# Ten of 32 adaLN blocks moved from the conv-FFN stages into five gaps between stages

## The reference

```python
c_act = jax.nn.silu(c)
for l in range(DEPTH):
    mod = c_act @ ada_w[l] + ada_b[l]                 # 1024 x 6144 for each of 2 layers
    sh1, sc1, gt1, sh2, sc2, gt2 = [m[:, None, :] for m in jnp.split(mod, 6, axis=-1)]
    h = rms_norm(x, norm1_g[l]) * (1.0 + sc1) + sh1
    ...
```

## Time and profile before

| | us |
|---|---|
| median of 3 runs | 2023.67 (2022.28 to 2025.08) |
| profiled execution, its own time | 2017.43 |
| its span | 2015.7 |
| PE busy | 1856.9 (92%) |
| DVE busy | 1292.1 (64%) |
| ACT busy | 1025.2 (51%) |
| granted clock of PE, mean | 0.957 |
| one pair in the conv-FFN loops, from one adaLN block to the next (856.70 to 874.65 on PE) | 17.95 |
| products in a row, start to start (874.10, 874.22, 874.33, 874.44 on PE) | 0.113 |
| unit 0 of the LRU ends (ACT's first read of it starts at 605.95) | about 605.7 |

### The profile page before, as it was taken

The page is one execution under the profiler, slowest core; times in us unless marked ns, Lnnn a source line. Parts: engine busy times, 40 slices in busy tenths (PEclk is TensorE's granted clock), DMA queues, the critical chain, the costliest instruction groups (busy, mean ns, idle before and its releaser), DMA issues.

```text
span 2015.7 us, 40167 instructions
## 1 busy us (share of the span) xinstructions
PE 1856.9 (92%) x16293; PEld 1749.0 (87%) x16293; DVE 1292.1 (64%) x1985; ACT 1025.2 (51%) x1550; POOL 29.5 (1%) x48
## 2 busy tenths in 40 slices
PE   6999889999979579999979999889998999988998
PEld 5987879999969569999969899879997999987998
DVE  5845667777757467777765866655555766765554
ACT  5634455555556645555545465434443655444443
POOL 0000000000000000000000000000000000100000
PEclk9996899999989789999989999989999999998999
DMA  7540337777744227777623341225553433043553
GB/s 278 187 146 1 126 110 278 259 268 272 262 160 149 84 103 262 270 270 263 248 105 107 128 163 44 90 99 188 189 194 118 147 137 136 3 147 126 189 189 124
DMA packets 43886, 333.52 MB, mean 165 GB/s; under 512 B 4864, under 2 KB 4992, under 8 KB 5632
## 3 DMA queue, kind: packets, MB, share of 16 engines
q1 hardware_dynamic: 38592, 277.89, 38.3%
q0 software_dynamic: 4608, 50.33, 6.7%
q10 hardware_dynamic: 576, 3.71, 0.5%
HBM read 330.86 MB, written 1.05 MB: 165 GB/s over the span
## 4 chain that ended last, share of the span: by engine, by line
PE 85%; DVE 8%; ACT 4%; issue 2%; DMA 1%; DVEq 0%; ACTq 0%
PE unit L492 15%; PE unit L494 15%; PE unit L493 15%; PE acc L492 8%; PE acc L494 8%; PE acc L493 8%; PE misc L388 2%; PE misc L1328 2%; ACT w_hi L469 1%; PE acc L1420 1%; DVE w_lo L476 1%; DMA par<-par_in 1%; PE misc L1434 1%; DVE tmp L1618 1%; DVE tmp L1654 1%
## 5 line engine op out<-in xcount | busy, mean ns | idle before, releaser
L476 DVE TENSOR_TENSOR w_lo<-raw,w_hi 128x1024 fp32r<-128x1024 f32 x526 | 640.1, 1224 | 473.1 <-ACT w_hi L469 463.2
L469 ACT ACTIVATE w_hi<-raw 128x1024 fp32r<-128x1024 f32 x526 | 555.4, 1062 | 654.0 <-PE unit L494 385.0
L492 PE MATMUL unit<-h_hi,w_hi 128*128 128x256 f32 x2656 | 754.3, 284 | 50.1 <-DVE h_lo L403 32.9
L493 PE MATMUL unit<-h_lo,w_hi 128*128 128x256 f32 x2656 | 746.7, 281 | 0.0
L494 PE MATMUL unit<-h_hi,w_lo 128*128 128x256 f32 x2656 | 746.2, 281 | 0.0
L492 PEld LDWEIGHTS unit<-h_hi,w_hi 128*128 128x128 f32 x2656 | 509.8, 192 | 60.6 <-issue 42.2
L493 PEld LDWEIGHTS unit<-h_lo,w_hi 128*128 128x128 f32 x2656 | 510.7, 192 | 0.2
L494 PEld LDWEIGHTS unit<-h_hi,w_lo 128*128 128x128 f32 x2656 | 510.2, 192 | 0.0
L492 PE MATMUL acc<-mv_hi,w_hi 128*128 128x256 f32 x1360 | 384.7, 283 | 36.1 <-DVE mv_lo L548 36.1
L493 PE MATMUL acc<-mv_lo,w_hi 128*128 128x256 f32 x1360 | 380.2, 280 | 0.0
L494 PE MATMUL acc<-mv_hi,w_lo 128*128 128x256 f32 x1360 | 379.9, 279 | 0.0
(11 more groups left out here) (368 smaller groups left out, 1735.1 us busy)
## 6 DMA issues: line engine op xcount, KB each, us to landing
raw<-w_in SPq DMA_DIRECT2D x263, 1024.0 KB, 4.8
ada_ring<-ada_in POOLq DMA_DIRECT2D x32, 1536.0 KB, 8.5
keep<-gates_in ACTq DMA_DIRECT2D x1, 1280.0 KB, 5.4
par<-par_in ACTq DMA_DIRECT2D x1, 1261.0 KB, 14.6
x<-x_in SPq DMA_DIRECT2D x1, 1024.0 KB, 5.7
out<-x SPq DMA_DIRECT2D x4, 256.0 KB, 2.1
con<-con_in ACTq DMA_DIRECT2D x1, 950.0 KB, 4.7
con<-con_in ACTq DMA_DIRECT2D x1, 130.0 KB, 5.9
```

The lines of the kernel that those rows point to most:

```text
L469: act(half(w_hi, c, k), raw[c % RAW][:, CW // 2 * k:CW // 2 * (k + 1)], ACT.Copy).then_inc(S("high_parts"), 1)
L476: tt(half(w_lo, c, k), raw[c % RAW][:, CW // 2 * k:CW // 2 * (k + 1)], half(w_hi, c, k).bitcast(f32), ALU.subtract).then_inc(S("chunk_spli ...
L492: mm(out, w, m, start=first, stop=False)
L493: mm(out, w, ml, start=False, stop=False)
```

## The change

- Blocks 0 and 1 stand before `ffn0`, 16 and 17 before the LRU, 20 and 21 before `ffn1`, 30 and 31 before `in2_0`: on PE the first of each right behind the `pe_norm` of the result, in `misc[1]` (`pe_gap`), the second behind the `pe_norm` of the next stage's input, in the first bank of `acc` (`pe_gap_end`); on DVE both right behind the last `h_lo` (`dve_gap`).
- Blocks 18 and 19 stand in the LRU, on PE between its last input chunk and the first down chunk, in `misc[0]` and a bank `unit`; on DVE behind the last split of `lru_out`. There `dve_mod(0)` stands too, which was behind `dve_pre` of `ffn1`.
- `ffn0` keeps blocks 2 to 15 (one in each pair of the loop). `ffn1` keeps 22, before the first down chunk, and 23 to 29, one in a loop turn, in its first pair; the second pair has none.
- POOL's loop over loads is written out, with a table of slots (`SLOT`).

```diff
 pe_ffn:
             pe_unit(pe, c0 + 1, n0 + 1)
-            if l == 0:
-                pe.wait_ge(S("c_act"), 1)
-            pe_ada(pe, l, 0)
             for j in range(2):
                 pe_unit(pe, c0 + 2 + j, n0 + 2 + j)
-            pe_ada(pe, l, 1)
+            pe.wait_ge(S("ada_turned"), GAP[f"ffn{l}"] + 2)
+            if l == 1:
+                pe_ada(pe, 22, misc[0])
             pe_down(pe, c0 + 4, b0, True, False)
             with pe.Fori(0, 7) as i:
                 for k in range(2):
                     for j in range(2):
                         pe_unit(pe, c0 + 5 + 3 * k + j, n0 + 4 + 2 * k + j, i, 6, 4)
-                    pe_ada(pe, l, 2 + k, i)
+                    if l == 0:
+                        pe_ada(pe, 2 + k, misc[k], i)
+                    elif k == 0:
+                        pe_ada(pe, 23, misc[1], i, 1)
                     pe_down(pe, c0 + 7 + 3 * k, b0 + 1 + k, False, False, i, 6, 2)
...
 dve_ffn:
+            dve_gap(dve, f"ffn{l}")
             dve.wait_ge(S("unit_free"), U0[f"ffn{l}"] + 2)
...
                 product(2 * p + 1, i)
-                dve_ada(dve, l, p, i)
+                if l == 0 and p >= 2:
+                    dve_ada(dve, p, misc[p % 2], i)
+                elif l == 1 and p == 1:
+                    dve_ada(dve, 22, misc[0])
+                elif l == 1 and p == 2:
+                    dve_ada(dve, 23, misc[1], i, 1)
...
 pe_lru:
             pe_mod(pe, 0)
+            pe_ada(pe, 18, misc[0])
+            pe.wait_ge(S("unit_free"), n0 + 11)
+            pe_ada(pe, 19, unit[n0 % 2])
             pe_out(pe, "lru_out")
...
 dve_lru:
+            dve_gap(dve, "lru")
             dve.wait_ge(S("lam_log"), 1)
...
             dve_out(dve, "lru_out", lru_pair, recur)
+            dve_mod(dve, link, 0)
+            dve_ada(dve, 18, misc[0])
+            dve_ada(dve, 19, unit[n0 % 2])
             done_after(dve, END["lru_out"] - 1)
...
+        GAP = {"ffn0": 0, "lru": 16, "ffn1": 20, "in2": 30}
+        def pe_gap(pe, first, second):
+            n = GAP[second]
+            pe_norm(pe, first)
+            if n == 0:
+                pe.wait_ge(S("c_act"), 1)
+            if n == 20:
+                pe.wait_ge(S("mod_done"), 1)
+            pe_ada(pe, n, misc[1])
+        def pe_gap_end(pe, second):
+            pe_ada(pe, GAP[second] + 1, accb[0])
+        def dve_gap(dve, second):
+            n = GAP[second]
+            dve_ada(dve, n, misc[1])
+            dve_ada(dve, n + 1, accb[0])
...
 tensor program:
-            pe_norm(pe, "mix_post0")
+            pe_gap(pe, "mix_post0", "ffn0")
             pe_norm(pe, "ffn_pre0")
+            pe_gap_end(pe, "ffn0")
             pe_ffn(pe, 0)
```

More of the change, by code:

```diff
@@ L348, in one @@
             return con[0:rows, CON[name]:CON[name] + 1]
+        accb = [acc[:, 512 * b:512 * (b + 1)] for b in range(4)]
         ident, ones = cn("ident"), cn("ones")
@@ L1148, in pe_lru @@
             pe.wait_ge(S("gates_loaded"), 16)
+            pe.wait_ge(S("ada_turned"), 18)
             for k in range(5):
@@ L1307, in ada_load @@
             pool.dma_start(ada_slot[s], src).then_inc(S(f"ada_loaded{s}"), 16)
+        SLOT = [n % 2 for n in range(22)] + [0] + [1] * 7 + [0, 1]
+        TURN = [SLOT[:n].count(SLOT[n]) + 1 for n in range(2 * ADA_N)]
         def pool_ada(pool):
-            for s in range(2):
-                ada_load(pool, s, s)
-            with pool.Fori(0, ADA_N - 1) as i:
-                for s in range(2):
-                    pool.wait_ge(S("ada_rows"), i * 2 + (s + 1))
-                    ada_load(pool, s, i * 2 + (2 + s))
@@ L1319, in pe_ada @@
-        def pe_ada(pe, l, p, i=None):
-            n = ADA_N * l + p
-            pe.wait_ge(S(f"ada_loaded{n % 2}"), at(i, 16, 16 * (n // 2 + 1)))
-            if i is not None or n >= 2:
-                pe.wait_ge(S("ada_turned"), at(i, 2, n - 1))
+            for n in range(2 * ADA_N):
+                s = SLOT[n]
+                if TURN[n] > 1:
+                    before = max(m for m in range(n) if SLOT[m] == s)
+                    pool.wait_ge(S("ada_rows"), before + 1)
+                ada_load(pool, s, n)
@@ L1326, in pe_ada @@
+        def pe_ada(pe, n, bank, i=None, per=2):
+            s = SLOT[n]
+            pe.wait_ge(S(f"ada_loaded{s}"), at(i, 16, 16 * TURN[n]))
+            if i is not None:
+                pe.wait_ge(S("ada_turned"), at(i, per, n - per + 1))
             for k in range(8):
                 g = 32 * (k % 4)
-                ins = mm(misc[n % 2][g:g + 32, 0:ADA_W], cact[:, k:k + 1].to_broadcast([P, 32]),
-                         ada_slot[n % 2][:, k, :], start=(k < 4), stop=(k >= 4))
+                ins = mm(bank[g:g + 32, 0:ADA_W], cact[:, k:k + 1].to_broadcast([P, 32]),
+                         ada_slot[s][:, k, :], start=(k < 4), stop=(k >= 4))
@@ L1330, in pe_ada, with dve_ada @@
             ins.then_inc(S("ada_rows"), 1)
-        def dve_ada(dve, l, p, i=None):
-            n, w = ADA_N * l + p, ADA_W // 32
-            dve.wait_ge(S("ada_rows"), at(i, 2, n + 1))
+        def dve_ada(dve, n, bank, i=None, per=2):
+            w = ADA_W // 32
+            dve.wait_ge(S("ada_rows"), at(i, per, n + 1))
             if i is not None or n >= 1:
-                dve.wait_ge(S("ada_cols"), at(i, 2, n))
-            nc.vector.transpose(ada_turned[:, :], misc[n % 2][:, 0:ADA_W]).then_inc(S("ada_turned"), 1)
-            dve.wait_ge(S("ada_turned"), at(i, 2, n + 1))
-            dst = ada_cols[:, w * n:w * (n + 1)] if i is None else ada_cols[:, bass.ds(i * (2 * w) + w * n, w)]
+                dve.wait_ge(S("ada_cols"), at(i, per, n))
+            nc.vector.transpose(ada_turned[:, :], bank[:, 0:ADA_W]).then_inc(S("ada_turned"), 1)
+            dve.wait_ge(S("ada_turned"), at(i, per, n + 1))
+            dst = ada_cols[:, w * n:w * (n + 1)] if i is None else ada_cols[:, bass.ds(i * (per * w) + w * n, w)]
@@ L1389, in build @@
         oacc = acc8[:, 4:8, :]
-        accb = [acc[:, 512 * b:512 * (b + 1)] for b in range(4)]
         KB = [unit[0][:, :], unit[1][:, :], misc[0][:, :], misc[1][:, :]]
@@ L1424, in pe_b2_in @@
             pe_norm(pe, f"pre1_{l}")
+            if l == 0:
+                pe_gap_end(pe, "in2")
             c0, n0 = CH0[f"in2_{l}"], U0[f"in2_{l}"]
             pe_unit(pe, c0, n0, h_count=4 * HU[f"pre1_{l}"])
+            pe.wait_ge(S("ada_turned"), 32)
             pe.wait_ge(S("mod_done"), l + 1)
@@ L1571, in dve_b2_in @@
             dve_modulated(dve, link, f"pre1_{l}", l, 0)
+            if l == 0:
+                dve_gap(dve, "in2")
             ahead(dve_split, dve, c0)
@@ L2442, in _ @@
             pe_ssd(pe)
-            pe_norm(pe, "mix_post0")
+            pe_gap(pe, "mix_post0", "ffn0")
             pe_norm(pe, "ffn_pre0")
+            pe_gap_end(pe, "ffn0")
             pe_ffn(pe, 0)
-            pe_norm(pe, "ffn_post0")
+            pe_gap(pe, "ffn_post0", "lru")
             pe_norm(pe, "mix_pre1")
+            pe_gap_end(pe, "lru")
             pe_lru(pe)
-            pe_norm(pe, "mix_post1")
+            pe.wait_ge(S("ada_turned"), 20)
+            pe_gap(pe, "mix_post1", "ffn1")
             pe_norm(pe, "ffn_pre1")
+            pe_gap_end(pe, "ffn1")
             pe_ffn(pe, 1)
-            pe_norm(pe, "ffn_post1")
+            pe_gap(pe, "ffn_post1", "in2")
             for l in range(2):
@@ L2529, in _ @@
             dve_pre(dve, "ffn_pre1", block1("ffn_pre", 1))
-            dve_mod(dve, link, 0)
             dve_ffn(dve, 1, link)
```

2 lines of the change are left out of this document (1 added, 1 removed).

## The result

| us | before | after |
|---|---|---|
| median of 4 runs each | 2022.97 (2018.23 to 2025.08) | 1999.39 (1995.75 to 2007.97) |
| ratio, with its 95% interval | | 0.9893 [0.9854, 0.9931] |
| profiled execution, its own time | 2017.43 | 2007.97 |
| its span | 2015.7 | 2006.1 |
| granted clock of PE, mean | 0.957 | 0.962 |

The kernel is faster by 1.1%: 14 to 30 us by the interval. A second set of six runs of the same kernel (`r1_change`) gave 0.9917 [0.9885, 0.995], so 10 to 23 us. The profiled execution happens to be the slowest of its four; its parts are therefore read stage by stage, and beside the profile of `r1_change` (span 1997.3).

What follows compares the result with a forecast made beforehand. PE was taken to bound the kernel, busy 1856.9 of 2015.7 us. Removed blocks (3.2 + 2.8 + 1.1 = 7.1 us) plus 2 us of clock gave 9 us, so 2014.6 us was predicted, range 2006 to 2020.

Steps and rivals of the forecast that it cites:

- The price of a block, 1.64 us: In `ffn1`'s loop, a block costs PE 1.64 us if nothing else makes the down chunk wait.
- Of 1.53 us, 1.08 becomes a wait for DVE; 0.45 us comes back: At `ffn1`'s second-pair down chunks, DVE's `w_lo` wait replaces most of each removed block; seven blocks give 3.2 us.
- rival 1: Blocks come back whole, since DVE's chain moves up with PE: 17.4 us gained, 2006.3 us; chance 0.10.
- Prologues, 2.8 and 1.1 us: Blocks removed before the loops give 2.8 us in `ffn0`, 1.1 in `ffn1`, after some 0.5 of wait at unit 3.
- PE and DVE in the gaps, waits and loads, 0: Moved blocks and transposes fit idle time between stages; new PE waits and POOL's loads cost nothing: 0 us.
- The clock, 2 us: Over unit 0 of four stages, filled gaps lessen PE's clock falls: 2 us gained, of 6 at most.
- rival 2: PE's clock stays high in all gaps: 6 us from the clock, 13 us in all, 2010.6 us; chance 0.12.
- Rival 3, the transposes: DVE's transposes ahead of first splits are exposed, costing 7.8 us: 2022.4 us, no change; chance 0.15, including worse clock falls.
- rival 4, dear blocks: A block in a gap loses its overlap and takes 7.9 us: 36 us lost, 2051 us; chance 0.03.

Runs made afterwards that it cites:

- r2_no_ten: The changed kernel with the ten moved blocks left out on PE and DVE: 2005.22 us, ratio 0.9919 to before.
- r5_dve_late: The changed kernel with two unused DVE additions (about 2.4 us) ahead of the suspected split in each second pair of `ffn1`'s loop: 2003.44 us, ratio 0.9911 to before.
- r4_twice: The changed kernel with PE making each of the eight blocks of the four gaps twice, same output: 2000.66 us, ratio 0.9907 to before.
- r3_no_pe: The changed kernel with only the ten blocks' products on PE left out, DVE's transposes and copies kept: 2006.72 us, ratio 0.9924 to before.
- r8_before_fill: The kernel before, no block moved, with ten idle products behind each norm of the four gaps: 2013.12 us, ratio 0.9966 to before.

## Why the prediction was wrong

- **The price of a block, 1.64 us:** right. 1.62 by the turn of `ffn1`; 16 us (11 to 22) for ten by `r2_no_ten`.
- **"Of 1.53 us, 1.08 becomes a wait for DVE; 0.45 us comes back":** this is the step that failed. The loop gave 7 × 1.62 = 11.3 us instead of 3.2, and the down chunk waits for nothing. I gave the split at 874.27 to the down chunk because it came last before it in time, and took the earlier trace rows for the proof. Neither shows which chunk a split is for; the code does (two buffers, refilled in the order of the chunks). The rows at 869.32 and 870.42, which I gave to a unit, are the down chunk's own split, done 2.9 us before the units end; that at 874.27 is the next chunk's, whose step on ACT stands at 872.04. `r5_dve_late` shows it: 2.4 us more ahead of this split cost nothing. Put right, the term adds 8.2 us and the sum is 17.2, near rival 1's 17.4, which gave 2006.3. I gave that case 0.10.
- **Prologues, 2.8 and 1.1 us:** right. Unit 3 waits for its bank: the view says 0.23 us, but that counts from the end of a product that lasts 0.28. From start to start (298.59, 299.09, 299.31 in the changed kernel) the step is 0.50 and the next 0.22, where both are 0.11 otherwise, so 0.5 us are lost, as forecast. From the first sum of the gap to the first block of the loop, `ffn0` lost 2.3 us (59.9 to 57.6): 2.8 for the blocks and 0.4 for the faster unit 0, less 0.9 for the far spacing of the products behind unit 3's wait (last section). `ffn1` lost nothing there (60.9 to 61.5), since its first norm fell to the low clock for 3.0 us; without that it would be 2.4 shorter. In `r4_twice`, where it stays high, it is 58.3.
- **PE and DVE in the gaps, waits and loads, 0:** right (`r2_no_ten`, `r3_no_pe`). A load now takes 7.5 us to land instead of 8.5.
- **The clock, 2 us:** near in size, and that is luck in part. Up to the end of unit 0 the four gaps were 1.4 and 1.6 us shorter in the two profiles, but so were the empty gaps of `r2_no_ten` (2.0; in `r3_no_pe` they were 0.6 longer), so no run shows that the single blocks earned it. Unit 0 runs at the high level in two of four stages, as rival 2 had it, for which I allowed 6 us in all; but the falls moved to `ffn1`'s first norm and took 3.0 back. What rival 2 allowed came only with longer fills: 6.5 us in `r8_before_fill` (3 to 11 by its runs), and 1.4 to 4.8 in the four kernels with doubled blocks. The Trainium skill (TensorE: Matmul & The Clock Gate, "What's actually happening") says that activity releases the throttle. By that rule the trace of `r8_before_fill` agrees, with 1.00 in all four windows; in the changed kernel, with shorter fills, 0.80 and 0.71 are left in two of them.
- **Rival 3, the transposes, and rival 4, dear blocks:** both fall; 0.68 us of cover are left where it was thinnest, and a block in a gap lasts 1.50 us.
- **The range:** its low end was put at the whole-blocks case and left no room for what runs of this kernel scatter by. Its own ten runs lie between 1995.75 and 2016.61. That scatter hardly showed in the three runs of before (2022.28 to 2025.08; later ones went from 2014.17 to 2037.01), and the last section shows one source of it. Even with the failed step put right the forecast would be 2006.4, 7 us above the first median and 3 above the second (2003.38).

Summed up: whole blocks (16.4 less 1.0 of waits in the prologues) and 1 to 2 us in the gaps make some 17 us; the stages `ffn0` to `in2_0` show 16.2 and 16.7, and the two sets of runs gave 21.6 and 16.8 by their ratios, with 17 in both intervals. What makes the first set 5 us better isn't shown.

## What to carry to other kernels

A wait with a name is not yet a wait on the path: before it is priced, count through the buffers which piece of work the named signal serves, and look at a place where the supposed cover is missing. If the trace doesn't show one, a few microseconds of useless work ahead of the suspect tell it in one run. Small work of a busy engine goes well into its idle times of a few microseconds between dependent steps: here 1.5 us, and even 2.8, fitted for nothing into 3.3, and with 2.8 us or more unit 0 ran at the high clock in at least three of the four stages. Filler that is longer than the idle time is paid for: 15 idle products ahead of the last down chunk instead of 8 left `ffn0` 1.9 us longer (309.5 against 307.6).
